# Second mixer: score passes of the two attention maps alternate, mLSTM score passes stand between value products, and ScalarE takes eight PSUM evictions from VectorE

## The reference

```
h    = rmsnorm(x); proj = h @ w_in -> dq, dk, dv, mq, mk, mv, mo, mi, mf
# four attention heads with two maps each (64 rows of q and k for a map)
s_c  = dq_c . dk_c / 8, causal;  p_c = softmax(s_c)          (c = 0, 1)
o_diff = (p_0 - lam * p_1) @ dv; rmsnorm over the head's 128 columns
# four mLSTM heads: q, k of 64 columns after a causal convolution and silu
scores = (q . k) * exp(gates);  num = scores @ v;  den = sum(scores)
hm = rmsnorm(num / max(|den|, floor)) * sigmoid(mo)
x = x + rmsnorm(concat(o_diff, hm) @ w_out)
```

## Time and profile before

| | |
|---|---|
| median of three runs | 1635.49 us (1631.95 to 1636.21) |
| profiled execution, its own time | 1633.56 us |
| its span | 1631.8 us |
| PE busy | 1580.8 us (97%), 7230 matmuls |
| DVE busy | 789.3 us (48%) |
| ACT busy | 580.8 us (36%) |

### The profile page before, as it was taken

One profiled execution on the slowest core, in us unless ns is written; L12 is line 12 of the kernel. 1 busy time (PEld: TensorE's weight loads), 2 busy tenths in 40 slices (PEclk: granted clock), 3 DMA queues, 4 the chain that ended last, 5 costly groups with the idle time before them and its releaser, 6 DMA issues.

```text
span 1631.8 us, 19453 instructions
## 1 busy us (share of the span) xinstructions
PE 1580.8 (97%) x7230; PEld 1279.7 (78%) x7230; DVE 789.3 (48%) x1155; ACT 580.8 (36%) x960; POOL 87.7 (5%) x74
## 2 busy tenths in 40 slices
PE   7999999999999999999999989899999999999998
PEld 5888888878867788888888868667777788888886
DVE  6444422455365564444323455687654643234424
ACT  5223212234245533232222263354643434224322
POOL 2000000001012120000000041100000000000000
PEclk9999999999999999999999999999999999999999
DMA  5333343333211133333333333321222232233232
GB/s 161 103 90 103 90 104 90 103 103 110 78 49 40 43 104 101 92 100 93 100 93 100 94 91 91 105 64 42 63 71 101 84 94 97 97 92 101 90 103 91
DMA packets 246028, 147.69 MB, mean 91 GB/s; under 512 B 17472, under 2 KB 230096, under 8 KB 245840
## 3 DMA queue, kind: packets, MB, share of 16 engines
q1 hardware_dynamic: 232896, 141.58, 29.1%
q10 hardware_dynamic: 13072, 5.31, 1.3%
HBM read 142.66 MB, written 4.21 MB: 90 GB/s over the span
## 4 chain that ended last, share of the span: by engine, by line
PE 87%; DVE 8%; ACT 3%; issue 1%; DMA 1%; POOL 0%; DVEq 0%; ACTq 0%; SPq 0%
PE bank L347 28%; PE bank L351 27%; PE bank L350 27%; DVE w_low L1086 3%; ACT w_high L595 1%; DVE region L1097 1%; ACT region L600 1%; PE bank L2037 1%; DMA w_raw<-in_w_out 0%; PE bank L2320 0%; PE bank L1944 0%; ACT sq L608 0%; DVE d_s L1421 0%; DVE c_acc L1444 0%; PE bank L2025 0%
## 5 line engine op out<-in xcount | busy, mean ns | idle before, releaser
L347 PE MATMUL bank<-region,w_high 128*128 128x512 f32 (+1 forms) x1484 | 588.1, 396 | 18.7 <-DVE w_low L1086 11.5
L351 PE MATMUL bank<-region,w_low 128*128 128x512 f32 (+1 forms) x1484 | 579.5, 391 | 0.0
L350 PE MATMUL bank<-region,w_high 128*128 128x512 f32 (+1 forms) x1484 | 579.2, 390 | 0.0
L1086 DVE TENSOR_TENSOR w_low<-w_raw,w_high 128x1024 fp32r<-128x1024 f32 (+1 forms) x259 | 336.1, 1304 | 149.4 <-ACT w_high L595 145.3
L595 ACT CAST w_high<-w_raw 128x1024 fp32r<-128x1024 f32 (+1 forms) x259 | 265.6, 1028 | 261.3 <-DMA w_raw<-in_ffn_w_down 107.4
L347 PEld LDWEIGHTS bank<-region,w_high 128*128 128x128 f32 (+1 forms) x1484 | 278.8, 188 | 91.1 <-DVE w_low L1086 15.5
L351 PEld LDWEIGHTS bank<-region,w_low 128*128 128x128 f32 (+1 forms) x1484 | 278.6, 188 | 60.1
L350 PEld LDWEIGHTS bank<-region,w_high 128*128 128x128 f32 (+1 forms) x1484 | 279.0, 188 | 56.3
L347 PE MATMUL bank<-w_high,region 128*128 128x512 f32 x416 | 168.2, 404 | 8.3 <-DVE rope_y L1387 3.5
L351 PE MATMUL bank<-w_high,region 128*128 128x512 f32 x416 | 165.1, 397 | 0.0
L350 PE MATMUL bank<-w_low,region 128*128 128x512 f32 x416 | 165.0, 397 | 0.0
(11 more groups left out here) (257 smaller groups left out, 1315.9 us busy)
## 6 DMA issues: line engine op xcount, KB each, us to landing
w_raw<-in_ffn_w_down SPq DMA_DIRECT2D x48, 512.0 KB, 3.9
w_raw<-in_ffn_w_gate SPq DMA_DIRECT2D x44, 512.0 KB, 3.7
w_raw<-in_ffn_w_up SPq DMA_DIRECT2D x44, 512.0 KB, 3.7
w_raw<-in_w_in SPq DMA_DIRECT2D x40, 512.0 KB, 3.8
w_raw<-in_w_up SPq DMA_DIRECT2D x32, 512.0 KB, 4.0
w_raw<-in_w_down SPq DMA_DIRECT2D x32, 512.0 KB, 3.5
w_raw<-in_w_out SPq DMA_DIRECT2D x16, 512.0 KB, 3.8
region_f<-in_x SPq DMA_DIRECT2D x4, 512.0 KB, 5.8
```

Source lines behind the costliest of these rows:

```text
L347: mm = pe.matmul(out, a_hi, b_hi, start=start, stop=False)
L350: pe.matmul(out, a_hi, b_lo, start=False, stop=False)
L351: return pe.matmul(out, a_lo, b_hi, start=False, stop=stop)
L1086: last = dve.tensor_tensor(piece(w_low[b % RING]), piece(w_raw[b % RING]), piece(w_high[b % RING]).bitcast(F32), ALU.subtract)
```

## The change

- `d_scores` now makes both maps of one w in one call: pass 0 of map 0, pass 0 of map 1, pass 1 of map 0, and so on. The number and shape of the matmuls is the same.
- `m_scores` is split into single passes, and `m_values` into single triples. In an iteration PE now runs pass 0, triple 0, pass 1, triple 1, pass 2, triple 2 (as many triples as there are), then triple 3 if j = 3. What stood between scores and value products (L2152 at u = 1, the turn of rstd at u = 4, the spreads at u = 6, 8, 10, 12) now stands behind the last of them.
- `d_copy` and `value_raw` move from DVE to ACT, with the same data and semaphores. The copy stands right behind the square; `value_raw` stands at the head of w = 11, 13, 15 and 19.

```diff
@@ ACT
                 act.activation(sq[:, h % 2, :], bank[h % 2][:], ACT.Square).then_inc(e_sq, 1)
+                act.copy(o_diff[:, h, :], bank[h % 2][:]).then_inc(e_copied, 1)
+            def value_raw(k):
+                act.wait_ge(acc_ready, RES["mv"] + k + 1)
+                act.activation(mv_raw[:, k, :], bank[3][:], ACT.Identity, scale=r_col[:, TT + k:TT + k + 1]).then_inc(acc_free, 1)
...
+                if w in (11, 13, 15, 19):
+                    value_raw((11, 13, 15, 19).index(w))
@@ DVE
-            def d_copy(h):
-                dve.wait_ge(e_sq, h + 1)
-                dve.tensor_copy(o_diff[:, h, :], bank[h % 2][:]).then_inc(e_copied, 1)
-            def value_raw(k):
-                dve.wait_ge(acc_ready, RES["mv"] + k + 1)
-                dve.tensor_scalar(mv_raw[:, k, :], bank[3][:], r_col[:, TT + k:TT + k + 1], None, ALU.mult).then_inc(acc_free, 1)
@@ PE
-            def d_scores(u):
-                w, c = divmod(u, 2)
+            def d_scores(w):
...
+                for pass_ in range(3):
+                    for c in range(2):
+                        if pass_ == 0 and w >= 1:
+                            pe.wait_ge(e_biased, 2 * w + c - 1)
...
+                        mm = pe.matmul(bank[4 + c][:, 0:n], part[1][rows_, qt, q * P:(q + 1) * P], part[1][rows_, kt, 0:n],
+                                       start=pass_ == 0, stop=pass_ == 2)
...
+                for pass_ in range(3):
+                    if u < MH * TT:
+                        m_score_pass(u, pass_)
+                    if 2 <= u < MH * TT + 2 and pass_ <= (u - 2) % TT:
+                        m_value(u - 2, pass_)
+                if 2 <= u < MH * TT + 2 and (u - 2) % TT == 3:
+                    m_value(u - 2, 3)
...
-                if 2 <= u < MH * TT + 2:
-                    m_values(u - 2)
```

More of the change, by code:

```diff
@@ L1496, in _ @@
             for w in range(4 * DH + 8):
-                if w in (11, 13, 15):
-                    value_raw(w // 2 - 5)
                 if w < 4 * DH:
@@ L1509, in _ @@
                     turned_lo(w - 3, e_thi, e_tlo)
-                if w >= 11 and (w - 11) % TT == 0:
-                    d_copy((w - 11) // TT)
                 if w in (1, 3, 5, 7):
@@ L1518, in _ @@
                     convolve(w // 2 - 1)
-                if w == 19:
-                    value_raw(3)
                 if 11 <= w < 15:
@@ L2138, in _ @@
             values("dv", 0, after_dv)
-            def d_scores(u):
-                w, c = divmod(u, 2)
+            def d_scores(w):
                 h, q = divmod(w, TT)
[L2143 to L2147, removed]
+                n = (q + 1) * P
+                for pass_ in range(3):
+                    for c in range(2):
+                        if pass_ == 0 and w >= 1:
+                            pe.wait_ge(e_biased, 2 * w + c - 1)
+                        rows_ = slice(64 * c, 64 * c + 64)
+                        qt, kt = h + (8 if pass_ == 2 else 0), 4 + h + (8 if pass_ == 1 else 0)
+                        mm = pe.matmul(bank[4 + c][:, 0:n], part[1][rows_, qt, q * P:(q + 1) * P], part[1][rows_, kt, 0:n],
+                                       start=pass_ == 0, stop=pass_ == 2)
+                        if pass_ == 2:
+                            mm.then_inc(e_score, 1)
             def head_sums(dst, h, squares):
@@ L2170, in m_spread_max, with m_scores_ready @@
                 spread4(bank[0], h, max_rows).then_inc(m_bc, 1)
[L2172 to L2175, removed]
+            def m_scores_ready(u):
                 if u == 0:
@@ L2182, in m_scores @@
                     pe.wait_ge(m_prod, u - 1)
-                split3(pe, bank[4 + u % 2][:, 0:S - k * P], part[1][rows_, 8 + kt, k * P:(k + 1) * P], part[1][rows_, kt, k * P:(k + 1) * P],
-                       part[1][rows_, 8 + qt, k * P:], part[1][rows_, qt, k * P:], True, True).then_inc(m_score, 1)
-            def m_values(u):
-                h, j = divmod(u, TT)
[L2188 to L2196, removed]
-                out = bank[num_bank(h, j)][:, j % 2 * MV:(j % 2 + 1) * MV]
[L2198 to L2204, removed]
@@ new lines, in m_score_pass @@
+            def m_score_pass(u, pass_):
+                h, k = divmod(u, TT)
+                rows_ = slice(64 * (h % 2), 64 * (h % 2) + 64)
+                qt, kt = h // 2 + (0 if pass_ == 1 else 8), 2 + h // 2 + (0 if pass_ == 2 else 8)
+                mm = pe.matmul(bank[4 + u % 2][:, 0:S - k * P], part[1][rows_, kt, k * P:(k + 1) * P], part[1][rows_, qt, k * P:],
+                               start=pass_ == 0, stop=pass_ == 2)
+                if pass_ == 2:
+                    mm.then_inc(m_score, 1)
@@ new lines, in m_value @@
+            def m_value(u, k):
+                h, j = divmod(u, TT)
+                if k == 0:
+                    pe.wait_ge(m_plo, u + 1)
+                    if h == 0:
+                        pe.wait_ge(mv_lo_ready, j + 1)
+                    if j % 2 == 0:
+                        half = 2 * h + j // 2
+                        if half == 2:
+                            pe.wait_ge(e_copied, DH)
+                        if half >= 3:
+                            pe.wait_ge(m_ncp, half - 2)
+                out = bank[num_bank(h, j)][:, j % 2 * MV:(j % 2 + 1) * MV]
+                cols = slice((j - k) * P, (j - k + 1) * P)
+                w_hi_k, w_lo_k = weight_hi(TT * h + k)[:, cols], weight_lo(TT * h + k)[:, cols]
+                pe.matmul(out, w_hi_k, mv_hi[:, k, h, :], start=(k == 0), stop=False)
+                pe.matmul(out[:, 0:P], w_hi_k, mv_lo[:, k, P * h:P * (h + 1)], start=False, stop=False)
+                mm = pe.matmul(out, w_lo_k, mv_hi[:, k, h, :], start=False, stop=(k == j))
+                if k == j:
+                    mm.then_inc(m_pv, 1)
@@ L2232, in _ @@
                 if w < 4 * DH:
-                    d_scores(2 * w)
-                    d_scores(2 * w + 1)
+                    d_scores(w)
                     if w == 0:
@@ L2255, in _ @@
                         m_spread_max(u // TT + 1)
-                    m_scores(u)
+                    m_scores_ready(u)
+                for pass_ in range(3):
[5 more added lines that the diff above has]
+                    m_value(u - 2, 3)
+                if u < MH * TT:
                     if u == 1:
```

## The result

| | median | runs | ratio to before |
|---|---|---|---|
| before, first pairing | 1633.74 us | 4 | |
| changed | 1649.95 us (1645.91 to 1658.83) | 4 | 1.0108 (1.0088 to 1.0128) |
| before, on the chip of the last experiments | 1635.62 us | 18 | |
| changed, the same chip | 1652.62 us (1646.61 to 1656.33) | 6 | 1.0096 (1.0065 to 1.0128) |

The forecast was +8.4 us and 1643.9, range 1638.5 to 1649.0; measured were +16.2 and, on one chip, +17.0. The changed kernel's profiled execution took 1648.66 us (span 1646.9), 15.1 more than that of before.

What follows compares the result with a forecast made beforehand. PE was taken to bound the kernel, with 87% of the chain of waits. 8.0 + 0.4 + 0.6 + 0.7 - 1.0 - 0.3 = +8.4 us on 1635.49 gave 1643.9 us, range 1638.5 to 1649.

Steps and rivals of the forecast that it cites:

- The price of the new order: mLSTM stretch: score passes between value products add 24 switches to 64 rows, 8.0 us, plus smaller terms of 0.4, 0.6, 0.7.
- the steps on the mLSTM stretch: 8.0 for added switches, 0.4 for projections behind them, 0.6 for two spreads, 0.7 for the wait before unit 15's products.
- A visit: mLSTM iterations: one switch of PE to 64-row passes and back, 0.35 us, or 0.30 with 128 columns.
- The last wait: Unit 15's value products wait for DVE's low part; two triples no longer hide it, +0.7 us.
- ScalarE's part: Copies and evictions moved to ACT: PE's wait at the last attention turn goes, -1.0, and an eviction wait, -0.3 us.
- The 0 to 1.5 us set against it: Start of mLSTM stretch: ACT's added work delays the mo weight casts; taken as 0, range 0 to +1.5 us.
- The alternation: Attention scores: both maps' passes already overlap, so alternating them gives 0.0 us, bounds -0.1 to +0.3.
- the row that decided it: Attention scores in the trace before: both maps' passes start together, six passes of 512 columns in 0.89 us.
- the clock: mLSTM stretch: no added time at the lower granted clock in the forecast's sum; more such stretches were left to a rival.
- rival C: mLSTM stretch: thinner work brings two or three more stretches at the lower clock, +12 us, 1647.5; chance 0.11.
- The argument against C: mLSTM stretch: no piece at the lower clock fell between 1150.7 and 1201.3 in the profile before.
- One reading: Slow piece at 1147.30 before: eight matmuls took 3.3 us where they take 1.8, read as 1.6 us lost.

Runs made afterwards that it cites:

- e10: Changed kernel plus six matmuls of 252 columns in each of fourteen mLSTM iterations; 1649.88 us, ratio 1.0091 to before.
- e6: e1 plus six matmuls of 252 columns in each of iterations 2 to 15 of the mLSTM stretch; 1639.35 us, ratio 1.0039 to before.
- e8: Kernel before with only the alternating map passes of d_scores; 1634.45 us, ratio 1.0009 to before.
- e11: Kernel before with only value_raw and the copies moved to ScalarE; 1634.24 us, ratio 0.9983 to before.
- e1: Changed kernel with the mLSTM score passes and value triples put back into one block each; 1633.30 us, ratio 0.9983 to before.
- e5: e1 plus six matmuls of only 2 columns in each of iterations 2 to 15 of the mLSTM stretch; 1643.38 us, ratio 1.0062 to before.
- e9: Changed kernel run again, unedited, on the chip of the last experiments; 1652.62 us, ratio 1.0096 to before.
- e2: Kernel before with only the mLSTM interleaving of passes and triples; 1656.60 us, ratio 1.0108 to before.

## Why the prediction was wrong: the clock term

**The price of the new order was right.** The cleanest pair is e10 and e6: the same filler, both with the upper clock all through the stretch, interleaved and in blocks. 73.12 - 63.99 = 9.1 us, where the steps on the mLSTM stretch gave 8.0 + 0.4 + 0.6 + 0.7 = 9.7. A visit cost 0.35 us in the row shown. The last wait grew from 0.59 to 1.24 us (+0.7 expected).

**ScalarE's part was right.** -1.1 us between e8 and e11, and -1.4 between e8 and e1; -1.3 was expected. The 0 to 1.5 us set against it at the start of the mLSTM stretch did not come.

**The alternation was right** at 0.0 (e8), as was the row that decided it.

**The failed step is the clock.** The forecast gave it nothing, and put more pieces at the lower clock into rival C with a chance of 0.11 and +12 us in all. What came was C: 9.1 - 1.1 = 8.0 us from the steps, and +17.0 measured on one chip, so about 9 us are the clock's. The runs as a whole bear this out, not the profiled one alone: the median of span x (1 - clock) rose from 15.5 us in before to 26.4, by 10.9, and that of span x clock by 6.2. Part of the price may thus be nearer 6 than 8 us; the clock's term is the larger one either way. C had the mechanism, with too small a price. The argument against C, "none fell between 1150.7 and 1201.3 before", was weak. It said that before kept its clock there, not how near it was to losing it. The same prediction showed that the new order makes that stretch a sixth longer with the same columns, and it read the piece of the earlier trace rows as following a stretch of small products. e10 shows that the fall goes away when the same visits stand among denser work, and e5's profile that thin work added to that stretch can bring the clock down with no other change.

**The range was too narrow for the same reason.** The changed kernel's four first runs spread from 1645.9 to 1658.8 us, and their spans multiplied by their clocks lie within 1.6 us of each other (1623.9 to 1625.5). In the six of e9 the two spreads are 9.7 and 5.7 us. Before spreads as widely, from 1630.9 to 1646.0 us in 29 runs. How much of the lower clock an execution catches differs from run to run, so the term is not a number but a spread of some 10 us, and the range had 5 us of room above the forecast.

**One reading was off.** The prediction took the 3.3 us at the lower clock in before for 1.6 us lost. e8, with that stretch at the upper clock throughout, took 56.44 us against 56.79: 0.4 us. In e8 PE waited 1.0 us for ScalarE soon after that place, and in before it did not, so most of what the slow piece lost was probably time that PE did not need.

**Left open**: why e2 and the changed kernel, whose PE order differs only in `d_scores`, had some 31 and 11 us at the lower clock inside the stretch (worked out from 0.80 and 0.92). Runs of one kernel differ as much (e9's six lie between 18.1 and 31.4 in the last column's measure), and it was not tried further. e5 and e6 show that few columns are enough; by what the added visits bring the clock down, their 64 rows, their lone passes or the short pauses beside them, was not separated either.

## What to carry to other kernels

Count the changes between matmuls of 64 and of 128 rows as instructions with a price, here 0.35 us a visit, and group passes so that there are few. Two units in one visit saved 0.4 us where both lay in the same half of the partitions and 0.8 us for a pair in different halves, 2.9 us in all with the waits. Where PE is the bound, charge a rearrangement that lowers its work per microsecond twice, once for the gaps and once for the clock. The second charge is the more uncertain: compare every run's span times its clock, not medians alone. Before giving passes of independent partitions a new order to make them overlap, look whether their starts coincide already.

## What the runs showed of the hardware

- PE overlaps matmuls of different partition halves although they are not neighbours in program order: six passes of 512 columns in 0.89 us before, 0.90 with the maps alternating. The description of the engines at the start, by which each takes its own instructions in program order, is too simple for PE.
- Eighty-four matmuls more did not slow the changed kernel (1649.88 against 1652.62 us); the loss to the lower clock went down by 13 us with them.
- PE need not stand idle for its clock to fall. In e5's window at the lower clock it is busy for 10.10 of 10.10 us, and in the 6.2 us before that window (1153.58 to 1159.80) for 5.95: one wait of 0.3 us and then, behind a spread, 1.7 us of matmuls of 2 to 130 columns one behind the other. The Trainium skill, "TensorE: Matmul & The Clock Gate", section "A second HAM failure mode: psum-queue depth-cycling", tells of short idle pieces between groups of matmuls under which the clock goes down and up again. The changed kernel has such short pieces (0.09 us on each side of a visit), but e10 has them too and kept its clock in the stretch, so they are not shown to be the cause here. e5 and e6 show something that it does not tell of: with the same number of matmuls of 2 or of 252 columns the stretch had a clock of 0.93 or of 1.00.
- Six matmuls of 2 columns take little less time than six of 252. At the upper clock, from the start of the first to the projection behind the last, thin filler 0.64 us:

```profile
1158.49 0.78 PE L2280 MATMUL bank<-region 128*128 128x2 f32 x6
1159.13 0.48 PE L347 MATMUL bank<-region,w_high 128*128 128x512 f32 x1
```

and dense filler 0.75 us:

```profile
1165.70 0.91 PE L2280 MATMUL bank<-region 128*128 128x252 f32 x6
1166.45 0.40 PE L347 MATMUL bank<-region,w_high 128*128 128x512 f32 x1
```

At the lower clock six thin ones took 1.24 us (e5):

```profile
1165.69 1.38 PE L2280 MATMUL bank<-region 128*128 128x2 f32 x6
1166.93 0.77 PE L347 MATMUL bank<-region,w_high 128*128 128x512 f32 x1
```

so these take nearly twice as long at the lower clock, although they have hardly any columns.
